# A forgetting-attention stage: the rounded copy of the probabilities made by VectorE instead of a second exponential on ScalarE

## What is computed

```
log_f = log_sigmoid(f_logit + f_bias)
cum = cumsum(log_f)                       # per head, over the tokens
logits[t, s] = q_t . k_s / 8 + cum[t] - cum[s],  s <= t
p = softmax(logits, over s)
o_b = p @ v
y_b = o_b * silu(z_b)
```

## Time and profile before

| | |
|---|---|
| median of 3 runs | 1782.4 us (1780.52 to 1784.16) |
| the profiled execution | 1783.94 us, its span 1782.2 us |
| PE busy | 1645.5 us, 92% of the span |
| DVE busy | 934.7 us, 52% |
| ACT busy | 690.7 us, 39% |
| POOL busy | 670.9 us, 38% |
| ACT, exponentials into `p` (L1323) | 320 of 638 ns mean, 204.0 us |
| ACT, exponentials into `p_hi` (L1325) | 320 of 632 ns mean, 202.3 us |
| POOL, `p_lo` (L1369) | 320 of 1162 ns mean, 365.2 us |

### The profile page before, as it was taken

One profiled execution on the slowest core, in us unless ns is written; L12 is line 12 of the kernel. 1 busy time (PEld: TensorE's weight loads), 2 busy tenths in 40 slices (PEclk: granted clock), 3 DMA queues, 4 the chain that ended last, 5 costly groups with the idle time before them and its releaser, 6 DMA issues. The chain is left out here.

```text
span 1782.2 us, 23178 instructions
## 1 busy us (share of the span) xinstructions
PE 1645.5 (92%) x8226; PEld 1276.0 (72%) x8226; DVE 934.7 (52%) x1419; ACT 690.7 (39%) x1274; POOL 670.9 (38%) x561
## 2 busy tenths in 40 slices
PE   7699999999999999999659999999999999969986
PEld 5587878787878888888436667666676666657775
DVE  7255655555357668001435665565666656354444
ACT  0335454544311111311026566655665666620000
POOL 1012121212211111111127677866776777812222
PEclk9899999999999999999759999999999999979998
DMA  5133434242573333224562435252644432053433
GB/s 227 42 90 114 119 97 128 84 136 83 132 107 120 126 128 104 73 74 112 153 171 72 122 98 151 79 123 74 174 118 117 131 84 75 22 209 124 137 110 106
DMA packets 182846, 202.57 MB, mean 114 GB/s; under 512 B 45300, under 2 KB 129012, under 8 KB 179572
## 3 DMA queue, kind: packets, MB, share of 16 engines
q1 hardware_dynamic: 182740, 201.20, 39.6%
HBM read 125.92 MB, written 75.24 MB: 113 GB/s over the span
## 5 line engine op out<-in xcount | busy, mean ns | idle before, releaser
L501 PE MATMUL bank<-x_hi,w_hi 128*128 128x512 f32 x992 | 397.9, 401 | 18.4 <-POOL w_lo L524 14.3
L1369 POOL TENSOR_TENSOR m_p_lo<-m_p,m_p_hi 128x512 fp32r<-128x512 f32 (+1 forms) x320 | 365.2, 1162 | 80.1 <-ACT m_p_hi L1325 78.9
L501 PE MATMUL bank<-x_hi,w_lo 128*128 128x512 f32 x992 | 389.9, 393 | 0.0
L501 PE MATMUL bank<-x_lo,w_hi 128*128 128x512 f32 x992 | 389.3, 392 | 0.0
L1323 ACT ACTIVATE m_p<-m_st,m_fcol 128x512 f32<-128x512 f32 (+1 forms) x320 | 204.0, 638 | 238.8 <-PE m_st L1210 120.9
L524 POOL TENSOR_TENSOR w_lo<-w_raw,w_hi 128x1024 fp32r<-128x1024 f32 x33 | 93.1, 2820 | 514.5 <-ACT w_hi L591 505.2
L1435 DVE TENSOR_REDUCE m_maxima<-m_aux 128x1 f32<-128x512 f32 (+2 forms) x320 | 197.3, 622 | 141.4 <-PE m_aux L1181 96.0
L501 PEld LDWEIGHTS bank<-x_hi,w_hi 128*128 128x128 f32 x992 | 188.7, 190 | 55.7 <-POOL w_lo L524 14.8
L501 PEld LDWEIGHTS bank<-x_hi,w_lo 128*128 128x128 f32 x992 | 187.9, 189 | 40.7
L501 PEld LDWEIGHTS bank<-x_lo,w_hi 128*128 128x128 f32 x992 | 188.9, 190 | 37.0
L1325 ACT ACTIVATE m_p_hi<-m_st,m_fcol 128x512 fp32r<-128x512 f32 (+1 forms) x320 | 202.3, 632 | 0.0
(11 more groups left out here) (193 smaller groups left out, 2444.4 us busy)
## 6 DMA issues: line engine op xcount, KB each, us to landing
w_raw<-in_w SPq DMA_DIRECT2D x33, 512.0 KB, 3.9
dram_feat<-ring SPq DMA_DIRECT2D x48, 256.0 KB, 3.4
arena<-in_xT SPq DMA_DIRECT2D x8, 1024.0 KB, 5.8
arena<-dram_gates SPq DMA_DIRECT2D x32, 256.0 KB, 4.4
m_K<-dram_k_hi SPq DMA_DIRECT2D x16, 512.0 KB, 7.4
m_Q<-dram_q_hi SPq DMA_DIRECT2D x64, 128.0 KB, 3.4
o_y<-dram_mixT SPq DMA_DIRECT2D x16, 512.0 KB, 4.6
o_x<-in_x SPq DMA_DIRECT2D x16, 512.0 KB, 5.3
```

The lines of the kernel that those rows point to most:

```text
L501: mm = pe.matmul(banks[bank_of(s)][:], w[:, i % 2, k * P:(k + 1) * P], x[:, k, b * BLOCK:(b + 1) * BLOCK], start=(k == 0 and n == 0), stop ...
L1369: pool.tensor_tensor(p_lo[(s - 1) % PL][:, off:], p[(s - 1) % PL][:, off:], p_hi[(s - 1) % PH][:, off:].bitcast(F32), ALU.subtract).then_i ...
```

## The change

ACT no longer writes `p_hi`. DVE makes it at the head of its slot s, for unit s-1, by copying `p` (32 bit) into the rounded format. DVE waits for `p_ready` of the unit and for PE's use of the buffer. `scores(s)` now waits for `p` of unit s-3, not for `p_hi`. POOL still waits for `p_hi`. Line numbers behind the ACT part go down by two (L1369 is L1367), those behind the new DVE code go up by three.

```diff
@@ scores(s), PE
-                    done(pe, p_hi_ready, s - ST)
+                    done(pe, p_ready, s - ST)
@@ ACT
                     act.activation(p[s % PL][:, off:], st[s % ST][:, off:], ACT.Exp, bias=bias).then_inc(p_ready, 1)
-                    done(act, pv_done, s - PH)
-                    act.activation(p_hi[s % PH][:, off:], st[s % ST][:, off:], ACT.Exp, bias=bias).then_inc(p_hi_ready, 1)
@@ DVE
                 for s in range(END_SLOT + 1):
+                    if 0 <= s - 1 < N_UNITS:
+                        off = unit(s - 1)[3]
+                        dve.wait_ge(p_ready, s)
+                        done(dve, pv_done, s - 1 - PH)
+                        dve.tensor_copy(p_hi[(s - 1) % PH][:, off:], p[(s - 1) % PL][:, off:]).then_inc(p_hi_ready, 1)
                     if 0 <= s - LAG < N_UNITS and unit(s - LAG)[2] == 4 * unit(s - LAG)[1] + 3:
```

## The result

| | before | after |
|---|---|---|
| median | 1781.46 us (4 runs, 1776.01 to 1784.16) | 1822.14 us (4 runs, 1812.94 to 1824.04) |
| ratio | | 1.0222, 95% interval 1.0179 to 1.0265 |
| profiled execution, its span | 1783.94, 1782.2 us | 1823.04, 1821.0 us |

The change makes the kernel 41 us slower (1.8 to 2.7%). The forecast was 1801 us, 19 slower: the right side and inside the range, but less than half of the loss.

The account below looks back on a forecast made before the run. PE was taken to bound `mix`, 640 us for 320 slots, with POOL close behind. Short slots +4, waits +16 and ACT -1 summed to +19 us, 1801 against the median of 1782.4; range 1779 to 1838.

Parts of the forecast that it names:

- Clock: In `mix`, at a granted clock of 0.98: nothing to gain; a loss only if PE's gaps grow long.
- ACT is not waited for: In `mix`, dropping 320 ACT exponentials and freeing the score bank 0.69 us sooner gains only 1 us.
- The CAST's price: On DVE in `mix`, 0.42 us undisturbed per 512-column CAST, 123 us for all 320.
- CAST and POOL shut each other out: DVE's CAST and POOL's `p_lo` subtraction cannot run together; CAST mean nearer 0.8 us, `p_lo` clearly over 1301 ns.
- the queued turn: CAST and `p_lo` each ready when the other ends, seams overlapping: 1.43 us a full slot, 0.03 over PE's 1.40.
- a third of the turns bare: Where DVE's slot is filled, `p_lo` waits for a CAST that could not start before: 1.85 us a turn.
- Short full slots: 130 full `mix` slots without a DeltaNet chain step, 1.40 us each on PE, lengthened by 0.03: +4 us.
- Waits: PE's waits on DVE (7.4 + 1.8 us) and `p_lo` (1.7), together 10.9, growing by 2.5 to 27: +16 us.
- Faster: Rival: score bank freed early, CAST fitting inside POOL's idle time in `mix`: 1776 us, chance 0.10.
- hidden: Rival: a ring of three absorbs CAST and `p_lo` in the 2.41 us slots: 1782 us, within 3, chance 0.15.
- The bare turn: Rival: as the rule `p_lo` waits for a late CAST, 1.85 us a full slot: 1827, up to 1856; chance 0.17.
- The price without exclusion: Rival: copy at 0.68 us on DVE, POOL undisturbed, DVE's waits grow by about 10 us: 1792, chance 0.06.

Follow-up runs that it names:

- e4: Kernel before, but ACT makes the rounded copy `p_hi` out of `p` in SBUF instead of by a second exponential: 1782.9 us, 1.001.
- e14: Kernel before with values one slot later (LAG 4, more buffers) and ACT copying `p_hi` out of `p`: 1773.1 us, 0.9949.
- e5: Kernel before, ACT still writing `p_hi`, plus a DVE CAST of every `p` into a spare tile nobody reads: 1838.5 us, 1.0313.
- e6: Kernel before plus a spare DVE copy of every `p`, made by a maximum over one element instead of a CAST: 1807.1 us, 1.014.
- e9: The change, but the maximum reads only the first 128 columns of each tile: 1792.5 us, 1.0065.
- e13: The change with the maximum over only 128 columns and the copy made by a maximum over one element, not shutting POOL out: 1782.9 us, 1.0005.
- e2: The change, but DVE's copy is made by a maximum over one element, which does not shut POOL out: 1814.6 us, 1.0185.
- e10: Kernel before, but the maximum reads only the first 128 columns of each tile: 1774.1 us, 0.9949.
- e1: The change, but the CAST of unit s stands at the head of DVE's slot s instead of s+1: 1860.0 us, 1.0446.
- e11: The change with LAG 4 and its buffers, and the CAST at the end of DVE's slot, behind maxima and chain steps: 1839.1 us, 1.0319.

## Why the prediction was right on the side and wrong on the size

The forecast for the stage was 4 (short slots) + 16 (waits) - 1 (ACT) + 0 (clock) = +19 us. The accounts say +3.9 (rest), +18.0 (PE idle), +16.2 (clock) = +38.1.

- **Clock: "a loss only if PE's gaps grow long, kept for the upper end".** This is the step that failed: the term that the sum put at nothing. It measured +16.2 us, nearly as much as the waits themselves, and it is most of the difference between +19 and +38 in the stage. The profile before already showed 13.8 us lost to the clock beside 15.7 us idle (3.4 of the 13.8 in the first 20 us of the stretch, which begins at the lower level). I read the mean of 0.98 as "nothing there"; 0.02 of 640 us is 13. Nor is one long gap needed beside it: in the place shown above the clock fell around a gap of 2.2 us.
- **PE sets the pace, ACT is not waited for; -1 us.** Right. e4 and e14 show that the early bank and ACT's relief are worth nothing that can be measured.
- **The CAST's price, 0.42 us for a full tile.** Right for the undisturbed one: 69 full CASTs took 0.41 to 0.43 us, and the shortest of all (256 columns) took 275 ns where I had 0.28 us.
- **CAST and POOL shut each other out.** Right, and shown by taking it away: 31 us between e5 and e6, 9.7 between e9 and e13. I had expected it in both records; it is in DVE's (96 us in 320 CASTs), hardly in `p_lo`'s (+9 ns). I had said `p_lo` would be clearly longer: wrong.
- **"I take the queued turn as the rule", a third of the turns bare.** This reading was wrong too. I had argued that DVE has time to be a unit ahead of POOL. POOL waited for the CAST in 184 of 320 slots: DVE was behind, not ahead. I had named `finish`, the chain steps and doubled auxiliary items as what makes the CAST late, and put too few slots there. That the same CASTs hold up the maxima and the values' split, for which PE waits, I had written down as well, but the sum has it only in the factor of the waits. e6 measures that alone, without exclusion and without a late `p_hi`: +27 us, idle and clock together, for copies of 195 us by their records (DVE's busy time grew by 160, since records in a row overlap).
- **Short full slots, +4 us.** The rest term grew by 3.9 us, and that this is the same number is luck. The term stood for a turn of the pair 0.03 us too long in every short slot. Of 65 full-tile slots of 1.2 to 1.6 us that ran at full clock in both kernels, 60 agree within 0.03 us in both directions; the other five are 0.1 to 0.6 us longer. The pair's turn does not pace PE; single slots are held up. e2, whose copy does not collide, has a rest of 613.1 as well.
- **Waits, 10.9 to 27 us, +16.** Right in the sum, in part by offsetting errors. PE's idle time grew by 18.0 us. Of the three kinds of waits that I had named, 10.9 became 23.5 us: those on `p_lo` grew fivefold, 1.7 to 8.9, those on DVE by a factor of 1.6, 9.2 to 14.6, where one factor of 2.5 had stood for both.
- **The rivals.** Faster and hidden are out. The bare turn (1827) comes near in the time, and its mark, a stage longer by over 40 us, was nearly met with 38; but the short slots did not get longer, so it is not the turn that makes the time. The price without exclusion, 1792, was too low: e2 is that kernel and takes 1815.

What stays open: why the clock falls after some gaps and not after others (e9 has 22.0 us idle and loses 10.2, e2 25.4 and 27.0), and how the change's 41 us divide between exclusion and occupation exactly. e9, e10 and e13 divide 18.4 us into 9.7 and 8.8, e5 and e6 58.6 us into 31.4 and 27.2: about half each in both, but at other loads than the change's, and with a copy of 676 ns on the side without exclusion.

## What to carry to other kernels

Before work is moved to an engine that looks 60% busy, look at what stands behind it in that engine's order and who waits for that closely; here 320 copies of 195 us in all, put in front of the maxima with nobody waiting for the result, cost 27 us; and one slot sooner (e1) or the end of the same slot (e11) instead of its head cost 38 and 27 us more. If PE is the bound and its clock is not at 1.00 all through, price new idle time once for the wait and once more for the clock: in this kernel the second came to 0.45 to 1.25 times the first. And look for the few places where the wait arises: of 288 slots at full clock 222 did not change here at all. A copy between SBUF tiles on DVE is not free beside POOL: compare its shortest with its mean.

## What the runs showed that was not expected

- A CAST that nobody waits for costs more (58.6 us) than the same CAST on the path (41 us); it meets a running POOL instruction more often, and lengthens `p_lo` in 122 of 224 full tiles instead of 31.
- `mix` gains from one more slot between scores and values also without the change: 1774.7 us, 0.9965 (0.9951 to 0.998), PE idle 8.3 instead of 15.7 us. With ACT's copy in addition 1773.1, 0.9949 (0.9932 to 0.9966). Both beat the kernel before and the changed one.
- The short maximum shows how near DVE was to the path already before the change: 100 us less of its time (382.0 to 281.7) is worth 7.4 us (1781.5 to 1774.1) although DVE was idle for 40% of the stage.
